# First norm of a mixture-of-experts trunk: weight and offset applied after the dispatch

## The reference

```
m = hybrid_mixer(x, ...)                         # four mixers on one 1024 -> 2048 projection, then 1024 -> 1024
x = layer_norm(ALPHA * x + m, ln1_g[l], ln1_b[l])
f = grouped_moe(x, router_w, router_b, w_gate[l], w_up[l], w_down[l])
x = layer_norm(ALPHA * x + f, ln2_g[l], ln2_b[l])

def layer_norm(x, g, b):
    return (x - mean(x)) * rsqrt(var(x) + 1e-5) * g + b

def grouped_moe(x, ...):                         # 16 experts in 4 groups of 4; one router for both layers
    logits = x @ router_w
    best group by the sum of its two largest (logits + router_b); its two best experts, gates by softmax
    y = sum over the two experts of gate * ((silu(x @ w_gate[e]) * (x @ w_up[e])) @ w_down[e])
```

## Time and profile before

| | |
|---|---|
| median of 3 runs | 1986.54 us (1973.77 to 1989.5) |
| the profiled execution | 1980.59 us |
| its span on the slowest core (core 3) | 1979.5 us |
| spans of the eight cores | 1947.0 to 1979.5 us |
| busy: TensorE, VectorE, ScalarE, POOL | 1260, 1054, 647, 485 us |
| layer 0: mixer, then experts | to about 573, to about 942 us |
| layer 1: mixer, then experts, then the tail | to about 1502, to about 1850, to 1980 us |

### The profile page before, as it was taken

How to read it: one execution, slowest core, us unless ns; L and a number is a source line. 1 busy time by engine, 2 the same in 40 slices (tenths; PEclk the granted TensorE clock), 3 DMA queues, 4 the chain that set the end, 5 groups by cost and what they waited for, 6 DMA issues and landing times.

```text
span 1979.5 us, 24514 instructions; the slowest of 8 cores (1947.0 to 1979.5 us)
## 1 busy us (share of the span) xinstructions
PE 1260.2 (64%) x7136; PEld 651.6 (33%) x7136; DVE 1054.4 (53%) x2538; ACT 647.3 (33%) x1146; POOL 485.0 (25%) x357
## 2 busy tenths in 40 slices
PE   1668787865419698876064759695845968798200
PEld 0323333333205354543031324232423534455100
DVE  1266767586643233333279585858772422333596
ACT  1234554534302121111145454554532211221122
POOL 4012222213250000000865303031310000000597
PEclk8779897978659898988586879898966989899655
DMA  9955986989787999999983644693234999998563
GB/s 191 264 159 75 125 102 106 106 96 162 154 177 179 248 249 241 242 247 277 193 169 64 117 92 90 107 140 54 87 124 139 234 234 246 244 253 239 198 214 136
DMA packets 78770, 335.12 MB, mean 169 GB/s; under 512 B 10776, under 2 KB 22688, under 8 KB 62880
## 3 DMA queue, kind: packets, MB, share of 16 engines
q0 software_dynamic: 26384, 166.16, 49.5%
q1 hardware_dynamic: 52240, 167.23, 25.7%
HBM read 362.80 MB, written 147.19 MB: 258 GB/s over the span
## 4 chain that ended last, share of the span: by engine, by line
PE 33%; DMA 23%; issue 15%; DVE 15%; ACT 7%; POOL 3%; SPq 2%; DVEq 0%; another core or an unknown queue 0%; ACTq 0%; POOLq 0%
PE pb L596 31%; DMA s_xy<-xg 12%; DMA s_wbuf<-ew 3%; ACT s_scr L605 2%; DMA s_wbuf<-exp_w 2%; DVE s_scr L609 2%; DMA s_xtok<-x 2%; DMA yg<-s_scr 2%; SPq L406 2%; PE pT L1269 2%; ACT s_xtok L605 1%; ACT L605 1%; DMA s_xtok<-yg,s_gai 1%; DVE s_sm L675 1%; DVE s_scr L616 1%
## 5 line engine op out<-in xcount | busy, mean ns | idle before, releaser
L596 PE MATMUL pb<-s_xy,s_wbuf 128*128 128x352 bf16 (+3 forms) x3008 | 663.5, 338 | 111.6 <-ACT s_scr L639 27.8
L596 PEld LDWEIGHTS pb<-s_xy,s_wbuf 128*128 128x128 bf16 x3008 | 281.9, 101 | 348.7 <-issue 190.0
L596 PE MATMUL pb<-s_wbuf,s_xy 128*128 128x512 bf16 x792 | 255.9, 419 | 47.9 <-DVE s_xy L624 23.5
L596 PE MATMUL pb<-s_wbuf,s_scrb 128*128 128x512 bf16 (+1 forms) x768 | 240.2, 403 | 42.2 <-DMA s_wbuf<-ew 30.8
L616 DVE TENSOR_SCALAR s_scr<-pb,s_gsl 128x512 f32<-128x512 f32 (+1 forms) x192 | 135.1, 745 | 184.3 <-PE pb L596 130.7
L609 POOL TENSOR_TENSOR s_xtok<-s_xtok,s_lnp 128x1024 f32<-128x1024 f32 x68 | 166.4, 2449 | 172.8 <-ACT s_xtok L605 116.0
L1269 PE MATMUL pT<-s_identb,s_xy 128*128 128x128 bf16 (+1 forms) x768 | 139.5, 230 | 91.6 <-DMA s_xy<-xg 51.2
L641 ACT COPY s_xy<-pT 128x1024 bf16<-128x1024 bf16 (+1 forms) x96 | 90.3, 940 | 295.1 <-PE pT L1269 289.1
L609 DVE TENSOR_TENSOR s_scrb<-s_scr,pb 128x352 bf16<-128x352 f32 x128 | 63.8, 517 | 228.3 <-PE pb L596 228.0
L406 POOL DMA_DIRECT2D s_wbuf<-exp_w x42 | 22.4, 533 | 621.4 <-PE pb L596 537.4
L605 ACT ACTIVATE s_scr<-pb 128x352 f32<-128x352 f32 (+3 forms) x148 | 68.0, 475 | 288.7 <-PE pb L596 200.9
(11 more groups left out here) (121 smaller groups left out, 1670.4 us busy)
## 6 DMA issues: line engine op xcount, KB each, us to landing
ew<-exp_w POOLq DMA_DIRECT2D x36, 1536.0 KB
s_wbuf<-ew SPq DMA_DIRECT2D x54, 1024.0 KB, 17.4
s_wbuf<-exp_w POOLq DMA_DIRECT2D x42, 1024.0 KB, 14.3
yg<-s_scr SPq DMA_DIRECT2D x64, 512.0 KB, 15.8
s_xy<-xg SPq DMA_DIRECT2D x32, 516.0 KB, 12.8
yg<-s_scr SPq DMA_DIRECT2D x32, 384.0 KB, 21.3
xg<-s_gov SPq DMA_DIRECT2D x2, 5808.0 KB, 29.8
s_xtok<-x SPq DMA_DIRECT2D x17, 512.0 KB, 10.0
```

The costliest lines, as they stand in the source:

```text
L596: em.op(PE, lambda e: e.matmul(out.ap, lhsT.ap, rhs.ap, start=start, stop=stop), w=[out], r=[lhsT, rhs])
```

## The change

The norm's weight and offset are no longer applied ahead of the dispatch.

- `A_section` runs statistics and inverse root as before, and then a new step `sX`, which writes the normalised row (without weight and offset) as bf16 straight into `xrow`; transposes and copy follow as before. So `xy` and the rows in `xg` hold normalised values.
- The router takes the weight into its matrix (`rwb` = router weights times g) and adds `bcst` = b times the router weights to the logits. Both are made once per layer in `load_layer_params`: two more SP DMAs (router weights as f32 into `gtmp`, and `g1t`, weight and offset by channel), two multiplies, a 128-column matmul with ones into `B[5]`, a copy and a sum. The one load of `rwb` on POOL's queue at the start is gone.
- `x_turn` is cut by channel chunks: four turns of two chunks each, over all 352 rows, so that each chunk's weight and offset stand per partition; they are applied as the chunk leaves PSUM, two operations per turn, on ScalarE in turns 0 and 2 and on VectorE in turns 1 and 3.
- The old steps `sC` and `sD`, which make the residual for the second norm, are written behind expert e for tiles 2e and 2e+1 (tile 0 not in the last layer). `load_layer_params(l + 1)` is written behind expert 9 instead of 2.
- The scratch tile `scr` becomes a little smaller.

```
-        em.dma(POOL, rwb().ap.rearrange(...), rw_d.rearrange("(k p) n -> p k n", p=128), "dcp", w=[rwb()])
...
     def load_layer_params(l):
...
+            rwf, rwx, rwy = gtmp(0, 128), gtmp(128, 256), gtmp(256, 384)
+            em.dma(SP, rwf.ap.rearrange("p (k n) -> p k n", k=8), rw_d.rearrange("(k p) n -> p k n", p=128), "drw", w=[rwf],
+                   group_left=1)
+            em.dma(SP, g1t[l]().ap, g1t_d[l], "drw", w=[g1t[l]()])
...
+            tt(DVE, k16(rwb()), k16(rwf), kb(g1t[l](0, 8)), ALU.mult)
+            tt(DVE, k16(rwx), k16(rwf), kb(g1t[l](8, 16)), ALU.mult)
+            mm(B[5](0, 128), ones(), rwx, True, True)
+            cpy(DVE, rwy, B[5](0, 128))
+            em.op(DVE, lambda e: e.reduce_sum(out=bcst().ap, in_=rwy.ap.rearrange("p (k n) -> p n k", k=8), axis=AX.X),
+                  w=[bcst()], r=[rwy])
...
     def A_section(b):
-                pipeline(tiles, ln_stages(0) + xT_stages(alpha_after=True, pt_fixed=0, rows=xrow[b == nblk - 1]))
+                rows = xrow[b == nblk - 1]
+
+                def sX(r, i):
+                    act(rows[r](0, D), xtile(i), AF.Identity, bias=SMT(i, 15, 16), scale=SMT(i, 14, 15))
+                pipeline(tiles, ln_stages(0)[:2] + [sX] + xT_stages(pt_fixed=0, rows=rows)[1:])
...
     def R_section(b):
-                cpy(DVE, lg, col(0, n))
+                tt(DVE, v16(lg), v16(col(0, n)), e16(bcst()), ALU.add)
...
-            def x_turn(e, j):
+            def x_turn(e, q):
...
+                for kl in range(2):
+                    kc = 2 * q + kl
+                    for j in range(CT):
...
+                        dst = pT(kl * CAP + j * 128, kl * CAP + j * 128 + nj)
+                        em.op(PE, lambda e_, src=src, dst=dst, idn=idn: e_.transpose(out=dst.ap, in_=src.ap, identity=idn.ap),
+                              w=[dst], r=[src, idn])
+                for kl in range(2):
+                    kc = 2 * q + kl
+                    dst, src = xgT[s](kc * CAP, (kc + 1) * CAP), pT(kl * CAP, (kl + 1) * CAP)
+                    sc, bi = g1t[l](kc, kc + 1), g1t[l](8 + kc, 9 + kc)
+                    if q % 2 == 0:
+                        act(dst, src, AF.Identity, bias=bi, scale=sc)
+                    else:
+                        ts(DVE, dst, src, sc, ALU.mult, bi, ALU.add)
+                if q < CT:
...
-                    if e_ + 1 < NE and fc >= 1:
-                        x_turn(e_ + 1, fc - 1)
+                    if e_ + 1 < NE:
+                        x_turn(e_ + 1, fc)
...
-                if e_ == 2 and not last:
+                late = [i for i in (2 * e_, 2 * e_ + 1) if (1 if last else 0) <= i < NT]
+                for st_ in ln_stages(0)[2:]:
+                    for i in late:
+                        st_(0, i)
+                if e_ == 9 and not last:
                     load_layer_params(l + 1)
```

More of the change, by code:

```diff
@@ L485, in build @@
     rw_d = din("router_w", [D, NE])
+    g1t_d = din("g1t", [L, 128, 16])
     ew_d = din("exp_w", [L, NE, 128, 12288])
@@ L542, in build @@
         gtmp = sb("gtmp", 512)
+        g1t = [sb("g1t%d" % k, 16) for k in range(L)]
+        bcst = sb("bcst", NE)
         yT = lambda a, c: xy(8192 + a, 8192 + c)
@@ L547, in build @@
         XB0 = 7 * SW
-        scr = sb("scr", 768 + 4 * D)
+        scr = sb("scr", 7 * (NB + 30) + D)
         scrb = sb("scrb", 1536 + 4 * GW, BF16)
@@ L746, in build @@
         x_in(1)
-        em.dma(POOL, rwb().ap.rearrange("p (k n) -> p k n", k=8), rw_d.rearrange("(k p) n -> p k n", p=128), "dcp",
-               w=[rwb()])
         em.dma(POOL, identb().ap, ident_d, "dcp2", w=[identb()])
@@ L1259, in x_load @@
                        w=[xgS[s](2 * 1032, 3 * 1032)], r=[xgD.rows(0, 2000)])
-            def x_turn(e, j):
+            def x_turn(e, q):
                 s = e % 2
[L1263 to L1275, removed]
-                stt(DVE, gs_, gv[2], float(e * CAP), gv[1], ALU.is_equal, ALU.mult)
-                tt(DVE, gs_, gs_, gv[0], ALU.add)
@@ new lines, in x_turn @@
+                for kl in range(2):
[7 more added lines that the diff above has]
+                if q < CT:
+                    j, nj = q, ROWS[q]
+                    gv = [xgG[s](j * 516 + 512 + c, j * 516 + 513 + c).v(lambda ap: ap[0:nj, :]) for c in range(3)]
+                    gs_ = gsl(s * CT + j, s * CT + j + 1, 0, nj)
+                    stt(DVE, gs_, gv[2], float(e * CAP), gv[1], ALU.is_equal, ALU.mult)
+                    tt(DVE, gs_, gs_, gv[0], ALU.add)
@@ L1279, in build @@
             x_load(0)
             x_load(1)
-            for j in range(CT):
-                x_turn(0, j)
+            for q in range(4):
+                x_turn(0, q)
             yi = 0
@@ L1466 @@
     ew[:, :, :, 8192:] = f(exp_w_down).reshape(L, NE, 4, 128, D).transpose(0, 1, 3, 2, 4).reshape(L, NE, 128, 4096)
+    g1t = np.concatenate([f(ln1_g).reshape(L, 8, 128).transpose(0, 2, 1), f(ln1_b).reshape(L, 8, 128).transpose(0, 2, 1)], axis=2)
     shared = {
+        "g1t": np.ascontiguousarray(g1t),
         "pp": pp, "bc3": bc3, "lnp": lnp, "gmwT": gmwT, "pbd": pbd, "rbb": rbb, "ebase": ebase, "trash": trash,
```

8 lines of the change are left out of this document (7 added, 1 removed).

## The result

Over 20 runs each, the changed kernel took a median of 1998.62 us (1987.79 to 2029.5) against 1978.88 us (1968.33 to 2012.59) for the kernel before: a ratio of 1.0082, 95% interval 1.0054 to 1.0110. The forecast was 1977.3 us, 9 us faster; the kernel became 16 us slower. That is still inside the 1% that the prediction called no change, but it has the other sign, and the interval leaves no doubt about it for these two programs (run 3 shows how far it hangs on the planned order).

The account below looks back on a forecast made before the run. Bounds: in-order queues in mixers, bare latencies between mixer and experts, transfers in experts. Terms +3 - 3 - 3.8 + 3.4 - 3.8 - 5 = -9.2 us took the median 1986.54 to 1977.3 us; range 1950 to 2010.

Parts of the forecast that it names:

- Mixers: Both mixers: `sC` and `sD` leave the chain but stay as fillers on idle engines; -3 us, bounds -20 and +5.
- End of the mixer, layer 1: Last tile before layer 1's scatters: `sX` replaces `sC`, two `sD` and `sE` in the chain; -3.8 us, bounds 0 and -5.
- End of the mixer, layer 0: Mixer to experts, layer 0: 3.3 us won, lost as row loads wait on SP behind `wmT`; +3.4, bounds -3.3 and +31.
- First turn: First `x_turn` of each layer: four shorter turns, evictions alternating between ScalarE and VectorE; -1.9 us per layer, bounds 0 and -6 together.
- Prologue: Start of the kernel: VectorE waits for router weights loaded on SP, ahead of the `hbb` multiply; +3 us, bounds 0 and +14.6.
- Experts 1 to 15: Expert stages after the first expert: rows asked for some 3 us earlier; -5 us, bounds -55 and +14.
- rival 1: Expert stages: the row load was their bound, so its 55 us wait goes unreplaced; 1927 us, chance 0.15.
- Rival 2: Layer 0 to 1: SP's queue is blocked and row loads slide, +31, plus the prologue's upper end; 2016 us, chance 0.17.
- Rival 3: Whole kernel: the change doesn't do what it says, norm steps stay in the mixer; 0, 1986.5 us, chance 0.20.
- Tail: After the last layer: not touched by the change; 0 us.
- the rule that I set aside: Layer 0's mixer end: `wmT` waits for one `dgm` multiply at most, making that term -3.3, the sum below -15.9.

Follow-up runs that it names:

- run 3: Changed kernel replanned, with the planner's price of a hop between engines 0.14 instead of 0.12: 1997.54 us, median of four runs.
- run 2: Changed kernel with the deferred norm steps' multiplies and adds on VectorE alone: 1954.39 us, 0.9851 of the kernel before.
- run 4: The control: kernel before replanned, with the planner's price of a hop 0.14 instead of 0.12: 1993.5 us, 1.0059 of the kernel before.
- run 1: Changed kernel with the deferred norm steps held back to the expert stage by a true read of each expert's first product: 1954.35 us, 0.983 of the kernel before.
- run 5: Kernel before with its first norm's multiplies and adds on VectorE alone: 1966.35 us, 0.9862 of the kernel before.
- run 8: Kernel before with the last of four copies of layer 1's mixer weights held until expert 1's rows are loaded: 0.9963 of the kernel before.
- run 10: Kernel before with the last two of four copies of layer 1's mixer weights held until expert 1's rows are loaded: 0.9985 of the kernel before.
- run 6: Changed kernel with the deferred norm steps held to the expert stage and their multiplies and adds on VectorE alone: 1953.67 us, 0.9806 of the kernel before.
- run 7: Changed kernel with the old row turn, three turns by row group with one plain ScalarE copy each: 1.0077 of the kernel before.

## Why the prediction was wrong, step by step

- **Mixers, the step that failed**: "no engine loses work; they only leave the chain", -3 with an upper bound of +5 (and -3.3 and -3.8 at the ends). Measured +7.5 and +16.0 by the medians, -3.8 and +12.9 on cores 0 to 3, +4.4 and +16.1 between the shorter halves. That the steps stay in the mixers as fillers on idle engines was right; that a filler on an idle POOL costs nothing was not, since VectorE pays for it: 16 and 18 us more excess, and mixers of 535.2 and 551.9 once the fillers are off POOL (run 2). The row that told so was in the prediction: the earlier trace rows, `wmT` stretched to 14.63 us beside POOL. I used it for the one wait on SP and did not ask which other VectorE instructions run beside POOL's 68 steps. How much of the +16 is this and how much order stays open: the control moved that mixer by 10 us, and the replanned pair has equal mixers on cores 0 to 3 (541.7 and 565.0 against 543.9 and 564.7) with 18 us more excess in the second. That POOL's first-norm steps cost more than the whole loss is shown by runs 1, 2 and 5; that the 0.8% belong to the change and not to this one order is not shown (run 3).
- **End of the mixer, layer 1**, -3.8: measured -0.4; the lower bound of nothing ("fillers fill the gap") is what happened, and the chain shows the two fillers.
- **End of the mixer, layer 0**, +3.4 (-3.3 to +31): the sign was wrong. I kept the order of before, `wmT` stretched beside `dgm` with the router weights and the row loads behind it on SP. In the new order `wmT` ran ahead of `dgm` in 0.69 us, and no row load waited for it on core 3; the 14.63 us were those of cores 3, 5 and 7 alone (4.1 us on cores 4 and 6, 0.7 on cores 0 to 2 of the same trace). The wait that I had in mind does appear in run 2: on core 3 there `wmT` waits for its data until 538.84, and the router weights and then the row loads leave behind it, the latter at 540.83, 9.4 us after the last scatter. What had held the row loads at 572.95 was that the scatters landed late, behind one copy of mixer weights, and the next copy then held the first rows (runs 8 and 10). In the changed kernel POOL issued its copies some 30 us earlier (the last at 530 instead of 560 on core 3), a by-product of the new order. Most of that gain comes back in the expert stage whenever its transfers are the bound: all of it in run 10; in the changed kernel 8 of 21 us by the first expert matmul.
- **First turn**, -1.9 each: measured 6.1 to 2.2 us from first transpose to first product, -3.9 each. The product works through the channel chunks in order, so it needs only the first turn, not all four. I had added up all four. In layer 0 the stretched router multiply takes part of it back.
- **Prologue**, +3: measured nothing; the router weights left SP at 55.65 us (core 5), VectorE used them at 85.79, long after the `hbb` multiplies (the last at 64.04) that I had put behind them, and the first scatter came at 234.5 us instead of 234.8.
- **Experts 1 to 15**, -5: measured -0.5 in layer 1 and, in layer 0, what the earlier start gave back. That the rows' wait would go and another transfer take its place was right; rival 1 is out.
- **Rival 2** had the right sign and another mechanism: nothing on SP was late. **Rival 3** named the outcome on cores 0 to 3 (+0.9 us) as a sum of parts that were all but zero.
- **Tail**, 0: +3 us, in all kernels here whose order changed except runs 3, 4 and 8 (131.6 to 131.7), so it belongs to the order.

On the rule that I set aside: the Trainium skill (SBUF — State Buffer, § Who interferes with whom) says that a VectorE instruction with two SBUF inputs and a GpSimd instruction that reads SBUF exclude each other, and that the one that came second waits in full. The trace agrees in what is stretched: in the changed kernel on core 3, 36 row statistics, 10 residual adds with one input in PSUM and 7 evictions from PSUM ran beside a multiply or add of POOL and none was stretched, while all 6 of the 512-column multiplies of two SBUF tiles were. (The scale of `s_gtmp` above, with one tile and per-row scalars as inputs, is stretched too; the same section of the Trainium skill counts that form, under conditions, among those that can take both ports.) Beside norm steps it agrees with the length of one instruction too: of the 299 VectorE instructions on the eight cores that were stretched there by over 1.5 us, 291 waited through one POOL instruction. Beside the four `dgm` multiplies it agrees on some cores and not on others (last section), and the row that the prediction's sum went by, 14.63 us, was one of those on which it does not.

## What to carry to other kernels

An idle engine is not a free one: before steps are handed to POOL as fillers, look at what the two-input VectorE instructions beside POOL take, form by form; a duration that is several times that of its own kind elsewhere is the price, and in the chain it appears as "issue". A step taken off the chain but left to a planner comes back as a filler, even into the gap that its removal made; only a dependency holds it where it should run. What a change is worth under a planner is known only after both kernels have been planned in another way as well: one number in the planner turned the sign here. And a gap in front of a stage that is bound by transfers is worth less than its length, since what is in flight in the gap has to be carried in the stage.

## What I had not expected of the hardware

- A 128-column multiply on VectorE took 12.77 us beside four POOL multiplies of 13.87 us together, and 0.29 us in the prologue: it got no turn between them. The same multiply in run 2, also on core 3, waited for one of the four only:

```profile
538.89 15.46 POOL L612 TENSOR_TENSOR s_dgm<-s_identb,s_ppb 128x2048 bf16<-128x2048 bf16 x4 [6.49 <-DMA s_gtmp<-gmwT]
539.45 4.63 DVE L619 TENSOR_SCALAR s_lnp<-s_lnp 128x2048 f32<-128x2048 f32 x1
...
544.00 3.69 DVE L612 TENSOR_TENSOR s_gtmp<-s_gtmp,s_g1t 128x128 f32<-128x128 f32 x1
```

  In the kernels before, after and of run 2, VectorE waited for one multiply at a time wherever the first of the four had itself been held up by VectorE (4.1 to 4.6 us instead of 3.6: cores 4 and 6 before, cores 0 to 3 and 5 in run 2), and through three or four of them wherever it had to wait and the first had not been held up. Why is open.
- TensorE stood still for 2 to 9 us in mid-run in some mixers, on the cores of one half of the chip only, at the same few places of the program. Core 5 after, chain:

```profile
1296.89 8.57 another core or an unknown queue x2
```

  The matmuls ahead of it end at 1298.3, VectorE waits for their result until 1305.4, and no engine has a visible reason. The same program on cores 0 to 3 passes this place in 0.4 us. Such places turn up with most kernels here, in runs 5 to 8 on cores 0 to 3. On cores 4, 5 and 7 after, they lie where the scatters' packets are in flight, but the other cores pass them with scatters in flight too; what it is stays open.
